# Gate projection: the last six pairs of weight chunks by seven block products over two token groups of 368, and the first attention head loaded in the last pair

## The reference, cut to what matters

```python
xn   = rms_norm(x, g_attn)                 # 1024 prompt rows and 64 sample rows (plus 16 meta rows), width 1024
proj = xn @ w_in                           # pooling channels | q latent | kv latent | rope key | 2*1024 gate columns
u_pool, q_lat, c_kv, k_r, gate_logits = split(proj)
g_pool, g_att = split(sigmoid(gate_logits))
out  = x + (g_pool * (pooled @ w_pool_map * pool_scale) + g_att * attention) @ w_o
```

## Time and profile before

| what | value |
|---|---|
| median of 3 runs | 2064.13 us (2063.47 to 2064.33) |
| the profiled execution's own time | 2062.92 us |
| its span, first to last instruction | 2061.1 us |
| mean granted TensorE clock | 0.999 |
| TensorE busy | 2024.2 us, 98% of the span |
| gate chunks 6 to 19 in the chain of waits | 234.3 to 413.5 us |

### The profile page before, as it was taken

One profiled execution on the slowest core, in us unless ns is written; L12 is line 12 of the kernel. 1 busy time (PEld: TensorE's weight loads), 2 busy tenths in 40 slices (PEclk: granted clock), 3 DMA queues, 4 the chain that ended last, 5 costly groups with the idle time before them and its releaser, 6 DMA issues.

```text
span 2061.1 us, 35685 instructions
## 1 busy us (share of the span) xinstructions
PE 2024.2 (98%) x12489; PEld 1864.2 (90%) x12489; DVE 1273.0 (62%) x2492; ACT 856.5 (42%) x1691; POOL 551.8 (27%) x562
## 2 busy tenths in 40 slices
...
GB/s 173 83 104 84 63 85 85 100 90 154 107 82 78 73 70 67 65 67 70 63 66 71 40 233 63 38 25 60 63 41 41 41 41 41 47 75 41 41 41 87
DMA packets 146270, 152.41 MB, mean 74 GB/s; under 512 B 50710, under 2 KB 122118, under 8 KB 145101
## 3 DMA queue, kind: packets, MB, share of 16 engines
...
...
## 4 chain that ended last, share of the span: by engine, by line
PE 89%; DVE 6%; ACT 2%; issue 2%; DMA 0%; POOL 0%; SPq 0%; ACTq 0%; DVEq 0%
PE ps L105 16%; PE ps L2324 16%; PE ps L107 16%; PE ps L106 16%; PE ps L859 12%; PE ps L1755 2%; PE ps L819 2%; PE ps L1472 1%; PE ps L1714 1%; PE ps L1720 1%; PE ps L2413 1%; DVE pa_ntop L1319 1%; PE ps L776 1%; PE ps L869 1%; ACT pa_prob L1234 1%
## 5 line engine op out<-in xcount | busy, mean ns | idle before, releaser
L2576 DVE TENSOR_TENSOR t_m<-t_m,ps 128x512 f32<-128x512 f32 x256 | 171.9, 684 | 111.0 <-PE ps L107 111.0
L1828 ACT ACTIVATE sq<-ps 128x512 f32<-128x512 f32 x256 | 153.1, 598 | 204.4 <-PE ps L107 203.1
L105 PE MATMUL ps<-f_late_h 128*128 128x512 f32 x512 | 199.4, 389 | 4.0 <-DVE t_m L2576 4.0
L107 PE MATMUL ps<-f_late_h,f_late_l 128*128 128x512 f32 x512 | 199.4, 389 | 0.0
L106 PE MATMUL ps<-f_late_l,f_late_h 128*128 128x512 f32 x512 | 199.3, 389 | 0.0
L1915 DVE TENSOR_REDUCE ss<-sq 128x8 f32<-128x512 f32 x256 | 172.8, 675 | 0.0
L2429 POOL TENSOR_TENSOR f_bl<-f_x,f_bh 128x512 fp32r<-128x512 f32 x45 | 58.4, 1298 | 365.6 <-ACT f_bh L2419 365.6
L1913 DVE TENSOR_TENSOR g_attn_b<-ps,g_attn_b 128x64 f32<-128x64 f32 x256 | 56.7, 221 | 147.1 <-ACT sq L1828 145.5
L2519 ACT ACTIVATE f_late_h<-f_raw 128x2048 fp32r<-128x2048 f32 x15 | 28.8, 1919 | 220.5 <-PE ps L107 220.5
L105 PEld LDWEIGHTS ps<-f_late_h 128*128 128x128 f32 x512 | 96.1, 188 | 24.3 <-DVE t_m L2576 2.7
L107 PEld LDWEIGHTS ps<-f_late_h,f_late_l 128*128 128x128 f32 x512 | 96.1, 188 | 20.0
...
## 6 DMA issues: line engine op xcount, KB each, us to landing
...
```

Of the source, the lines that this page charges most:

```text
L105: nc.tensor.matmul(out, lh, rh, start=first, stop=False)
L107: return nc.tensor.matmul(out, ll, rh, start=False, stop=last)
L1828: nc.scalar.activation(sq[:, j % 2, :].rearrange("p (a n) -> p a n", a=2), ps[:, kn_bank(j):kn_bank(j) + 2, 0:HALF], ACT.Square).then_inc( ...
L2576: nc.vector.tensor_tensor(out, out, ps[:, 4 + p % 4, :], ALU.add).then_inc(S["y"], 1)
```

## The change

Chunks 0 to 7 stay as they were. The last six pairs are computed by `gate_pair(q)`, q = 0 to 5. A pair is a matrix of two chunks (columns) by two halves of the 1024 inner rows, and the first two token groups (368 each) are the two columns of blocks on the other side. Winograd's form of Strassen's scheme gives this 2x2 product with seven block products instead of eight; the sums on the token side (`r11`, `r12`, `r21`, `r22`, high and low parts t1 to t4, 128x4x368 each) are made once, the sums on the weight side (S1 to S4) for every pair. The third group (352) is done plainly, four units. So a pair is 11 calls of `unit`, each 4 inner blocks x 3 passes = 12 matmuls: seven of width 368 and four of width 352, 132 in all, where 144 were.

- Weights: both chunks of a pair now share one `m_raw`, which is loaded anew (two DMAs) when the last low part of the pair before is made and POOL has read it. `m_wh`/`m_wl` are cut in four slots of 128x4x128. S1 to S4 are added on POOL (`x1`, `x2`) and their low parts subtracted there: eight POOL tensor operations of 128x512 a pair, where POOL did none. A11, A21, A12, A22 are split by ACT and DVE.
- Results: the products are united by DVE, five adds of 128x368 a pair, and ACT applies the sigmoid in five pieces and copies one bank (`taken`).
- Tokens: DVE makes ten sums and four low parts of 128x1472 during chunks 6 and 7 and the first pair, ACT four high parts.
- The stores of the pool state move ahead of the loads of chunks 8 and 9 on the SP queue. `load_head` and `load_values` come after unit 3 of the last pair; their splits go into that pair.
- The last pair's pool products come two ahead of unit 11 and one behind it. TensorE waits for the last union before it leaves the stage.

The diff, cut to its core (eight blanks at the start of the lines are taken off):

```diff
--- before.py
+++ after.py
...
+    for c in (8, 9):
+        sp.wait_ge(M["wl"], c - 1)
+        sp.dma_start(raw[:, c % 2], w_all[:, :, cols[c]:cols[c] + P]).then_inc(mw_in[c % 2], 16)
+    for q in range(1, PAIRS):
+        sp.wait_ge(M["comb"], pool_of(q - 1, "x2 again"))
+        sp.wait_ge(M["wl"], 8 + 4 * q)
+        for c in (8 + 2 * q, 9 + 2 * q):
+            sp.dma_start(raw[:, c % 2], w_all[:, :, cols[c]:cols[c] + P]).then_inc(mw_in[c % 2], 16)
     sp.wait_ge(M["tailo"], 16 * (2 + NSEQ))
...
+    sp.wait_ge(M["proj"], unit_of(PAIRS - 1, 3))
+    sp.wait_ge(M["comb"], pool_of(PAIRS - 1, "S3"))
     load_head(nc, Q, T, E, 0)
...
+    def low_sum(q, name, slot, src):
+        pool.wait_ge(M["wh"], high_of(q, name))
+        nc.gpsimd.tensor_tensor(slot_l[slot], src[:], f32(slot_h[slot]), ALU.subtract).then_inc(M["comb"], 1)
+    def first_sums(q):
+        for i in range(2):
+            pool.wait_ge(mw_in[i], 16 * (5 + q))
+        nc.gpsimd.tensor_tensor(x1[:], part(1, 0), part(1, 1), ALU.add).then_inc(M["comb"], 1)
+        pool.wait_ge(M["comb"], pool_of(q, "x1"))
+        nc.gpsimd.tensor_tensor(x2[:], x1[:], part(0, 0), ALU.subtract).then_inc(M["comb"], 1)
+        low_sum(q, "S2", 0, x2)
+    def second_sums(q):
+        low_sum(q, "S1", 2, x1)
+        pool.wait_ge(M["comb"], pool_of(q, "S1"))
+        nc.gpsimd.tensor_tensor(x1[:], part(0, 0), part(1, 0), ALU.subtract).then_inc(M["comb"], 1)
+        nc.gpsimd.tensor_tensor(x2[:], part(0, 1), x2[:], ALU.subtract).then_inc(M["comb"], 1)
+    pool.wait_ge(M["pool_d"], 8)
+    pool.wait_ge(M["tailc"], 2)
+    first_sums(0)
+    keep(0)
+    second_sums(0)
+    for q in range(PAIRS):
+        low_sum(q, "S3", 0, x1)
+        low_sum(q, "S4", 3, x2)
+        keep(q + 1)
+        if q == PAIRS - 2:
...
+        if q + 1 < PAIRS:
+            first_sums(q + 1)
+            second_sums(q + 1)
+    pool.wait_ge(E["qk_hi"], 1)
+    nc.gpsimd.tensor_tensor(T["ql0"][:], T["raw_q"][:], f32(T["qh0"][:]), ALU.subtract).then_inc(E["q_lo"], 1)
+    keep(KD - 1)
...
+    def block_high(q, name):
+        src, slot, comb, unit = {
+            "S2": (x2[:], 0, "x2", 6 - UNITS), "S1": (x1[:], 2, "x1", 8 - UNITS), "A11": (part(0, 0), 1, "", 10 - UNITS),
+            "A21": (part(1, 0), 3, "", 0), "S3": (x1[:], 0, "x1 again", 1), "A12": (part(0, 1), 2, "", 3),
+            "A22": (part(1, 1), 1, "", 4), "S4": (x2[:], 3, "x2 again", 5)}[name]
+        for i in range(2):
+            act.wait_ge(mw_in[i], 16 * (5 + q))
+        if comb:
+            act.wait_ge(M["comb"], pool_of(q, comb))
+        if q == 0 and unit < 0:
+            act.wait_ge(M["proj"], 8 if name == "S1" else 7)
+        else:
+            act.wait_ge(M["proj"], unit_of(q, unit))
+        nc.scalar.activation(slot_h[slot], src, ACT.Copy).then_inc(M["wh"], 1)
...
+        act.wait_ge(kept[q % 2], 16 * (q // 2 + 1))
+        act.wait_ge(M["proj"], unit_of(q, 1))
+        nc.scalar.activation(g[:, 0, g1], ps[:, 3, 0:368], ACT.Copy).then_inc(M["taken"], 1)
+        if q == 0:
+            act.wait_ge(M["proj"], 8)
+            sum_high(3, 8, xh[:, 0:HK, g1], r12)
+        block_high(q, "S3")
+        block_high(q, "A12")
+        if q == 0:
+            act.wait_ge(M["tlow"], 3)
+            sum_high(4, 10, t4h[:], r21)
+        block_high(q, "A22")
+        block_high(q, "S4")
+        if q == PAIRS - 1:
+            act.wait_ge(E["w_in"], 16)
+            nc.scalar.activation(T["w_h0"][:], T["w_raw"][:], ACT.Copy).then_inc(E["w_hi"], 1)
+            act.wait_ge(E["raw_in"][0], 16)
+            nc.scalar.activation(T["qh0"][:], T["raw_q"][:], ACT.Copy).then_inc(E["qk_hi"], 1)
+            act.wait_ge(E["raw_in"][1], 16)
+            nc.scalar.activation(T["kh0"][:], T["raw_k"][:], ACT.Copy).then_inc(E["qk_hi"], 1)
+        act.wait_ge(M["proj"], unit_of(q, 7))
+        nc.scalar.activation(g[:, 0, g0], ps[:, 2, 0:368], ACT.Sigmoid).then_inc(M["taken"], 1)
+        act.wait_ge(M["proj"], unit_of(q, 8))
+        nc.scalar.activation(g[:, 0, g2], ps[:, 6, 0:352], ACT.Sigmoid).then_inc(M["taken"], 1)
+        act.wait_ge(M["u"], 5 * q + 3)
+        nc.scalar.activation(g[:, 1, g1], g[:, 1, g1], ACT.Sigmoid)
+        if q + 1 < PAIRS:
+            block_high(q + 1, "S2")
+            block_high(q + 1, "S1")
+        act.wait_ge(M["u"], 5 * q + 4)
+        nc.scalar.activation(g[:, 1, g0], g[:, 1, g0], ACT.Sigmoid)
+        act.wait_ge(M["proj"], unit_of(q, 10))
+        nc.scalar.activation(g[:, 1, g2], ps[:, 7, 0:352], ACT.Sigmoid).then_inc(M["taken"], 1)
+        if q + 1 < PAIRS:
+            block_high(q + 1, "A11")
+        act.wait_ge(M["u"], 5 * q + 5)
+        nc.scalar.activation(g[:, 0, g1], g[:, 0, g1], ACT.Sigmoid).then_inc(M["sig"], 2)
+        if q + 1 < PAIRS:
+            block_high(q + 1, "A21")
...
+    def union(q, out, left, bank, unit, before):
+        dve.wait_ge(M["proj"], unit_of(q, unit))
+        if before:
+            dve.wait_ge(M["u"], 5 * q + before)
+        nc.vector.tensor_tensor(out, left, ps[:, bank, 0:368], ALU.add).then_inc(M["u"], 1)
...
+    split_chunk(6)
+    sums(r11, h12, ((h11, ALU.subtract), (l12, ALU.add), (l11, ALU.subtract)))
+    dve.wait_ge(M["sig"], 1)
+    gated_pool(0, 0, 0)
+    gated_pool(0, 1, 1)
+    split_chunk(7)
+    sums(r22, h22, ((r11[:], ALU.subtract), (l22, ALU.add)))
+    sums(r12, h22, ((h12, ALU.subtract), (l22, ALU.add), (l12, ALU.subtract)))
+    sum_low(1, t1l[:], r11, t1h[:])
+    dve.wait_ge(M["tailo"], 16 * (2 + NSEQ))
+    sums(r21, h21, ((r22[:], ALU.subtract), (l21, ALU.add)))
+    gated_pool(0, 2, 2)
+    sum_low(2, t2l[:], r22, t2h[:])
+    block_low(0, "A11")
+    for q in range(PAIRS):
+        j = q + 2
+        g = gate[:, j % 2]
+        dve.wait_ge(M["taken"], taken_of(q, "copy"))
+        union(q, g[:, 0, g1], g[:, 0, g1], 2, 2, 0)
+        dve.wait_ge(M["sig"], 2 * j)
+        gated_pool(j - 1, 0, 0)
+        if q == 0:
+            block_low(0, "A21")
+            sum_low(3, xl[:, 0:HK, g1], r12, xh[:, 0:HK, g1])
+        block_low(q, "A12")
+        gated_pool(j - 1, 1, 1)
+        if q == 0:
+            sum_low(4, t4l[:], r21, t4h[:])
+        block_low(q, "A22")
+        union(q, g[:, 1, g1], g[:, 0, g1], 5, 6, 1)
+        gated_pool(j - 1, 2, 2)
+        union(q, g[:, 1, g1], g[:, 1, g1], 4, 3, 2)
+        if q == PAIRS - 1:
+            dve.wait_ge(E["qk_hi"], 2)
+            nc.vector.tensor_tensor(T["kl0"][:], T["raw_k"][:], f32(T["kh0"][:]), ALU.subtract).then_inc(E["k_lo"], 1)
+        union(q, g[:, 1, g0], g[:, 0, g1], 5, 9, 0)
+        if q + 1 < PAIRS:
+            block_low(q + 1, "A11")
+        else:
             dve.wait_ge(E["w_hi"], 1)
             nc.vector.tensor_tensor(T["w_l0"][:], T["w_raw"][:], f32(T["w_h0"][:]), ALU.subtract).then_inc(E["w_lo"], 1)
-            dve.wait_ge(E["qk_hi"], 2)
-            nc.vector.tensor_tensor(T["kl0"][:], T["raw_k"][:], f32(T["kh0"][:]), ALU.subtract).then_inc(E["k_lo"], 1)
+            dve.wait_ge(M["taken"], taken_of(PAIRS - 1, "C11"))
+            gated_pool(KD - 1, 0, 0)
+            dve.wait_ge(M["taken"], taken_of(PAIRS - 1, "rest0"))
+            gated_pool(KD - 1, 1, 2)
+        union(q, g[:, 0, g1], g[:, 0, g1], 4, 11, 0)
+        if q + 1 < PAIRS:
+            block_low(q + 1, "A21")
+    dve.wait_ge(M["sig"], 2 * KD)
+    gated_pool(KD - 1, 2, 1)
...
+    def unit(bank, slot, xs, width, start, stop):
+        for k in range(HK):
+            out = ps[:, bank, 0:width]
+            for n, (w, x) in enumerate(((slot_h[slot], xs[0]), (slot_h[slot], xs[1]), (slot_l[slot], xs[0]))):
+                last = nc.tensor.matmul(out, w[:, k, :], x[:, k, :], start=start and k == 0 and n == 0,
+                                        stop=stop and k == HK - 1 and n == 2, skip_group_check=True)
+        last.then_inc(M["proj"], 1)
+    def gate_pair(q):
+        b11, b21, b22, t3 = b_of(0, g0), b_of(1, g0), b_of(1, g1), b_of(0, g1)
+        rest = [b_of(0, g2), b_of(1, g2)]
+        j, lows = q + 2, 8 + 4 * q
+        pe.wait_ge(M["comb"], pool_of(q, "S2"))
+        if q == 0:
+            pe.wait_ge(M["tlow"], 2)
+            pe.wait_ge(M["sig"], 3)
+        else:
+            pe.wait_ge(M["taken"], taken_of(q - 1, "copy"))
+        unit(3, 0, (t2h, t2l), 368, True, True)
+        pe.wait_ge(M["wl"], lows + 1)
+        if q:
+            pe.wait_ge(M["taken"], taken_of(q - 1, "C11"))
+        unit(2, 1, b11, 368, True, False)
+        pooled(j - 1, 0, 0)
+        pe.wait_ge(M["comb"], pool_of(q, "S1"))
+        if q == 0:
+            pe.wait_ge(M["sig"], 4)
+        else:
+            pe.wait_ge(M["u"], 5 * q)
+        unit(4, 2, (t1h, t1l), 368, True, False)
+        if q:
+            pe.wait_ge(M["taken"], taken_of(q - 1, "rest0"))
+        unit(6, 1, rest[0], 352, True, False)
+        pooled(j - 1, 1, 1)
+        pe.wait_ge(M["wl"], lows + 2)
+        if q:
+            pe.wait_ge(M["taken"], taken_of(q - 1, "rest1"))
+        unit(7, 3, rest[0], 352, True, False)
```

(38 more changed lines are left out.)

112 lines of the change are left out of this document (76 added, 36 removed).

## The result

The changed kernel takes 2054.29 us in the median (five runs, 2052.49 to 2056.35), the kernel before 2064.13 (2063.06 to 2064.5). The ratio is 0.995, with a 95% interval of 0.994 to 0.9961: 9.8 us less. A second set on another chip gave 2055.57 against 2063.93, ratio 0.9957 (0.9943 to 0.9971): 8.4 us less. The forecast was 2055.1, with 2052.2 to 2060.0 as its range.

What follows compares the result with a forecast made beforehand. TensorE was taken to bound the gate stage, as long as weights keep coming. Terms -12.1 + 2.4 + 0.7 = -9.0 us took the median from 2064.13 to 2055.1, range 2052.2 to 2060.0.

Steps and rivals of the forecast that it cites:

- wait in the second pair: TensorE at the second pair's first matmul waits 2.4 us for weights reloaded late (0.9 to 3.9).
- Fewer matmuls: Gate stage: 72 matmuls fall away at 0.168 us each, 12.1 us less; upper end 13.4.
- Rival 4: Gate stage: the fewer matmuls are each slower as weights change, no gain above 0.18 us; 0.07 together with the POOL-bound rival.
- The first pair: Extra low and high parts delay A22 by 3.6 us; load issued at 273.0, taking 7.1; TensorE then waits 2.4.
- The steady ring: Reload, POOL sums and splits within a later pair finish 2.8 us before TensorE needs them; nothing paid.
- Rival 2: Every pair waits: slower load (-2.9) and POOL operations (-1.2) use up the slack; 2059 to 2063 us; chance 0.09.
- Rival 3: POOL bounds the gate stage, a loss above 2.4 us an operation; about 2074 us; 0.07 together with the slower-matmul rival.
- The start: Before the first pair at 258.8, DVE's sums and low parts end near 256.6, 2 us to spare; nothing paid.
- The end: Before attention, one pooled product beside drain, union and sigmoid: about 0.7 us more than before (0.3 to 0.9).
- The first head: Last pair: head loads issued after unit 3, splits covered by units 6 to 11; nothing paid.
- The clock: TensorE idle 3 of 10 us in the feed-forward part kept its clock at 1.00; nothing charged for a slower clock.

Runs made afterwards that it cites:

- experiment 3: Changed kernel with each pair's first unit computed twice into the same bank, so 144 matmuls a pair again: 2064.32 us, ratio to the kernel before 1.0001.
- experiment 4: Changed kernel with POOL computing x2 three times or once more than needed in pairs two to six: 2071.12 us (one run) with three, 2055.25 with one.
- experiment 5: Changed kernel with POOL issuing each pair's gate store only after the reload of both chunks has landed: 2055.01 us (single run).
- experiment 2: Changed kernel with TensorE's first prompt attention matmul no longer waiting for the last pair's gates (count 2H - 2 instead of 2H): 2055.85 us.

## Why the prediction was right

*The sum.* The stage gave 10.2 us, counted from chunk 6's start to attention (221.15 to 414.80 before, 221.37 to 404.80 after), against the 9.0 of the sum. By its own terms: 

| term | predicted | measured |
|---|---|---|
| 72 matmuls fewer | -12.1 (-13.4 as upper end) | -12.0 by experiment 3, -0.5 for the form with units: -12.5 |
| wait in the second pair | +2.4 (0.9 to 3.9) | +1.4, and 0.25 for the restart |
| end of the stage | +0.7 (0.3 to 0.9) | +0.5 (a wait of 0.61 where there was one of 0.1) |
| steady ring, start, first head, clock in the stage | 0 | 0 |
| sum | -9.0 | -10.35 by these terms, -10.2 as counted |

*Fewer matmuls:* right, a little small, as its own upper end had it. Units of 2.01 to 2.03 us and twelve of 368 with twelve of 352 in 3.91 to 3.95 were forecast as 2.02 and 1.93. Rival 4 is out.

*The first pair:* followed rightly link by link. The prediction had A22's low part at 272.9 and the load's issue at 273.0; the chain has 272.90 and 272.96. VectorE and POOL do take turns there, 1.1 us at xl and 1.1 at A22; without those turns, in experiment 3, the same two subtractions take 2.2 less. The Trainium skill (SBUF — State Buffer, Who interferes with whom) says that a VectorE instruction with two SBUF inputs and a GpSimd one shut each other out; the two rows of 1.68 and 2.78 for the same subtraction agree. The term that was mis-sized is the load: 7.1 us from the first load's issue to the second's landing was put in as the middle of 5.7 and 8.6, and it took 6.1 (272.96 to 279.04; the 5.66 of the chain are the second load alone). The upper end came from taking the 273 GB/s of one window for what the DMA engines can move. The wait was 1.0 shorter for it, 1.4 where the forecast looked for 2 to 3. The sum's miss of 1.2 is made of this 1.0, less the 0.25 of the restart that it did not have, 0.4 from the matmuls and 0.2 from the end; 0.1 stays open.

*The steady ring:* slack 2.8 forecast, 2.15 by experiment 4; nothing paid, and less to spare. Most of the difference is handing over: in the chain 0.04 to 0.15 us pass each time from one engine's end to the next one's start, which the sum put at nothing. Rival 2 put 4.1 us a pair against the slack, 2.9 of them from the store; experiment 5 leaves at most 0.4 of those. Rival 3 needed POOL operations of 2.4 us; they take 1.28 to 1.77 in the changed kernel's pairs. Added POOL work of 3.9 us a pair did bring the kernel to 2071, beyond the kernel before, so the mechanism of rival 3 exists; in pairs three to six it begins to cost at 2.15 us of added work, in the second at once.

*The start:* no wait of TensorE at 258.98; t2's low part was ready at 255.6, forecast 256.6. *The end:* size right, cause too simple: experiment 2 shows that the sigmoid is one link of a chain that goes on through the gated product and a cast to the first score. *The first head:* loads issued at 385.5, the last split (L958) ends at 399.6, 5.2 us ahead of attention. Covered; but VectorE's subtraction of its 1040 elements took 3.87 beside POOL's of 1024 with 2.41, longer than the sum's split times.

*The clock:* charged nothing, and in the stage it cost nothing: 1.00 from 258.98 to 404.80. The argument for it, that 3 idle of 10 us left the clock alone once, was weaker than it read: it is the same place in the feed-forward part, with the same wait of 2.3 us for VectorE, at which the changed kernel's profiled execution had its second fall. In the gate stage waits of 2.3, 1.8 and 5.2 us came with a fall, and waits of 2.5 and 1.7 did not. Had the wait come out at the 2.4 forecast, 1.6 us more might have been paid. That it cost nothing is in part luck.

*The median* was met within 0.8 us, but partly by two misses that offset: the stage gave 1.2 more than the sum, and in three of the first set's five runs the mean clock was 0.997 or 0.998, in the profiled one by falls that the prediction knew nothing of.
